# Decoder trunk on one core: where the down product of an expert item stands, how its weight buffers are given back, and in which order items are taken

## The reference, cut to what matters

```python
h = x + hybrid_mixer(rmsnorm(x), ...)            # three head groups and an output product
x = h + hierarchical_moe(rmsnorm(h), ...)
return rmsnorm(x)

# hierarchical_moe, t = 256 tokens of 2048, 4 groups of 8 experts
g_top, g_idx = lax.top_k(softmax(t @ rg_w + rg_b), 1)
e_top, e_idx = lax.top_k(softmax(e_logits), 2)
gate = one_hot(expert_id) * e_w                   # 2 of 32 experts for each token
h = silu(t @ w1[e]) * (t @ w3[e]) * gate[e]       # w1, w3: 2048 x 512
y = sum_e h @ w2[e]                               # w2: 512 x 2048
```

## Time and profile before

| | |
|---|---|
| median of 3 runs | 1461.44 us (1459.39 to 1463.98) |
| the profiled execution | 1461.95 us, its span 1460.2 us |
| mean granted clock of TensorE | 0.915 |
| busy share of the span | PE 82%, DVE 37%, ACT 24%, POOL 16% |
| DMA | 472.17 MB, mean 323 GB/s |

### The profile page before, as it was taken

How to read it: one execution, slowest core, us unless ns; L and a number is a source line. 1 busy time by engine, 2 the same in 40 slices (tenths; PEclk the granted TensorE clock), 3 DMA queues, 4 the chain that set the end, 5 groups by cost and what they waited for, 6 DMA issues and landing times.

```text
span 1460.2 us, 21576 instructions
## 1 busy us (share of the span) xinstructions
PE 1197.6 (82%) x8361; PEld 689.7 (47%) x8361; DVE 533.2 (37%) x1073; ACT 353.1 (24%) x651; POOL 229.7 (16%) x207
## 2 busy tenths in 40 slices
PE   8999999999998666578566667976889788789896
PEld 7874888977774122125112213322243234455563
DVE  6999312344436113114111212313132232344435
ACT  1120477565561101101101010211111111110003
POOL 2002766687860000000000000000000000000000
PEclk9999999999999888869867888999898899999999
DMA  8433444344486999999999999499867779999996
GB/s 210 171 132 139 162 174 172 116 168 139 156 345 268 427 429 429 426 428 427 428 428 426 428 429 426 185 410 428 340 263 329 316 332 422 427 426 430 430 426 286
DMA packets 71566, 472.17 MB, mean 323 GB/s; under 512 B 17329, under 2 KB 17410, under 8 KB 46274
## 3 DMA queue, kind: packets, MB, share of 16 engines
q1 hardware_dynamic: 70834, 469.75, 78.7%
q10 hardware_dynamic: 528, 1.05, 0.2%
q0 software_dynamic: 128, 0.26, 0.1%
HBM read 468.95 MB, written 2.10 MB: 323 GB/s over the span
## 4 chain that ended last, share of the span: by engine, by line
DMA 53%; PE 29%; DVE 2%; ACT 1%; POOL 1%; issue 1%; DVEq 0%; POOLq 0%; ACTq 0%
DMA ring<-in_expert_w_dram 53%; PE ps L1574 11%; PE ps L1916 8%; PE ps L1933 3%; PE ps L1894 2%; PE ps L1925 1%; POOL w_lo L569 1%; PE ps L1841 0%; PE ps L1866 0%; PE ps L1950 0%; DVE reg_x L1502 0%; DVE reg_y L1131 0%; PE ps L1748 0%; PE ps L1696 0%; PE ps L1906 0%
## 5 line engine op out<-in xcount | busy, mean ns | idle before, releaser
L569 POOL TENSOR_TENSOR w_lo<-ring,w_hi 128x512 fp32r<-128x512 f32 x152 | 200.0, 1346 | 72.4 <-ACT w_hi L631 71.2
L1933 PE MATMUL ps<-ring,reg_y 128*32 128x512 f32 x1248 | 174.9, 699 | 38.5 <-POOLq L594 26.7
L1404 DVE TENSOR_TENSOR y_lo_t<-ps,y_hi_t 32x512 fp32r<-32x512 f32 x156 | 107.1, 687 | 205.2 <-ACT y_hi_t L863 201.6
L863 ACT ACTIVATE y_hi_t<-ps 32x512 fp32r<-32x512 f32 x156 | 91.9, 589 | 323.8 <-PE ps L1933 320.9
L1393 DVE TENSOR_SCALAR reg_y<-ps,lamv 128x512 f32<-128x512 f32 x39 | 29.3, 750 | 319.9 <-PE ps L1916 319.9
L1916 PE MATMUL ps<-ring,reg_s 128*32 128x512 f32 x624 | 93.1, 724 | 59.2 <-POOLq L594 59.1
L1916 PE MATMUL ps<-ring,reg_y 128*32 128x512 f32 x624 | 90.2, 696 | 42.5 <-POOLq L594 42.2
L1916 PE MATMUL ps<-reg_e,reg_y 128*32 128x512 f32 x624 | 84.7, 665 | 42.6 <-POOLq L594 42.6
L1916 PE MATMUL ps<-reg_e,reg_s 128*32 128x512 f32 x624 | 86.5, 678 | 38.0 <-POOLq L594 38.0
L631 ACT ACTIVATE w_hi<-ring 128x512 fp32r<-128x512 f32 x152 | 91.6, 630 | 75.8 <-PE ps L1574 66.3
L1933 PEld LDWEIGHTS ps<-ring,reg_y 128*32 128x32 f32 x1248 | 39.3, 120 | 140.0 <-issue 78.1
(11 more groups left out here) (404 smaller groups left out, 1624.0 us busy)
## 6 DMA issues: line engine op xcount, KB each, us to landing
ring<-in_expert_w_dram SPq DMA_DIRECT2D x128, 2048.0 KB, 25.7
reg_e<-in_expert_w_dram SPq DMA_DIRECT2D x64, 2048.0 KB, 25.5
ring<-in_w_in_dram SPq DMA_DIRECT2D x19, 2048.0 KB, 8.1
ring<-in_w_out_dram SPq DMA_DIRECT2D x8, 2048.0 KB, 8.0
reg_x<-in_x_dram SPq DMA_DIRECT2D x4, 1024.0 KB, 8.6
ring<-in_w_in_dram SPq DMA_DIRECT2D x2, 1024.0 KB, 7.4
out_dram<-reg_x SPq DMA_DIRECT2D x3, 512.0 KB, 2.7
reg_e<-in_ssm_w_glu_dram ACTq DMA_DIRECT2D x1, 1024.0 KB, 8.9
```

The costliest lines, as they stand in the source:

```text
L569: G.tensor_tensor(w_lo[:, i % BUFS, :], unit(u % SLOTS_A)[:, c, :], w_hi[:, i % BUFS, :], ALU.subtract).then_inc(row_lo, 1)
L863: A.activation(y_hi_t[SLOT * q:SLOT * q + SLOT, 512 * k:512 * k + 512], psb[3][SLOT * k:SLOT * k + SLOT, :], cp).then_inc(e_yhi, 1)
L1404: V.tensor_tensor(y_lo_t[SLOT * q:SLOT * q + SLOT, w], psb[3][SLOT * k:SLOT * k + SLOT, :], y_hi_t[SLOT * q:SLOT * q + SLOT, w], ALU.subtr ...
L1933: last = M(psb[3][SLOT * i:SLOT * i + SLOT, :], hT[:, 2 * half + f, :], unit2(s)[:, f, 512 * i:512 * i + 512], start=half == 0 and f == 0, ...
```

## The change

There are four edits in the expert stage.

1. `down` of item n-1 no longer follows item n-1's own `turn`. It stands between the two up products of item n: w1 of n, down of n-1, w3 of n, turn of n. It keeps its old place, behind `gather`, at the end of a group and for a single item in the loop. The first item of a group's second block (`pe_item_behind`) has its eight pairs of `combine` behind that `down`, four of them behind `turn`.
2. `slot_free` becomes `w1_free`, `w3_free` and `w2_free`, with two counts for an item each, and `e_in` becomes `w1_in`, `w3_in` and `w2_in`. POOL passes landings on in PE's new order. SP's order of transfers stays.
3. The items that run singly (their number, `n_more` and one, known on the chip) come first, here items 0 to 6; the four fixed groups are items 7 to 38. The first gather and gates are for one item, not eight, and those in the loop too, where before they fetched eight. The last item is now the eighth of a group.
4. POOL clears `y_hi_t` and `y_lo_t` once before the expert stage. DVE's table of item experts (L1345) is put in `y_lo_t`. A small clearing of `selS` moves from the end to before the routing.

```diff
-                    sp.wait_ge(slot_free, n_ * 6 + k + 1)
+                    sp.wait_ge((w1_free, w3_free, w2_free)[k // 2], n_ * 2 + k % 2 + 1)
...
+            g.wait_ge(row_used, ROWS)
+            G.memset(y_hi_t[:, :].bitcast(F), 0.0)
+            G.memset(y_lo_t[:, :].bitcast(F), 0.0).then_inc(y_clear, 1)
...
+            landed(w1_in, 0, 0)
+            landed(w3_in, 2, 0)
             g.wait_ge(rk_ready, 2)
-            with g.Fori(1, ITEMS) as i_:
-                item_landed(g.value_load(ids[0:1, ds(i_, 1)], min_val=0, max_val=NE - 1))
+            more = g.value_load(n_more[0:1, 0:1], min_val=0, max_val=EXTRA - 2)
+            with g.Fori(0, more + 1) as x_:
+                landed(w2_in, 4, expert(x_))
+                e = expert(x_ + 1)
+                landed(w1_in, 0, e)
+                landed(w3_in, 2, e)
+            with g.Fori(0, GROUPS) as it:
+                for q in range(1, QG):
+                    n_ = it * QG + more + (q + 1)
+                    e = expert(n_)
+                    landed(w1_in, 0, e)
+                    landed(w2_in, 4, expert(n_ - 1))
+                    landed(w3_in, 2, e)
...
+            def pe_item_behind(i_, n_, h):
+
+                up(n_, QE * h, 0, (0, 1))
+                down(n_ - 1)
+                up(n_, QE * h, 1, (0,))
+                pe.wait_ge(e_stev, i_)
+                pe.wait_ge(e_ylo, n_ * 4 + 1)
+                combine(i_ - 1, (0, 1))
+                up(n_, QE * h, 1, (1,))
+                combine(i_ - 1, (2, 3))
+                turn(n_)
+                combine(i_ - 1, (4, 5, 6, 7))
                 slots_to_rows(i_, h)
...
+            def pe_group(i0, g_, n0, tail=False):
+                for q in range(QG):
                     n_ = n0 + q
+                    if q == 0:
+                        pe_item(i0, g_, n_)
+                    elif q % QE == 0:
+                        pe_item_behind(i0 + q // QE, n_, q // QE)
+                    else:
+                        up(n_, q, 0, (0, 1))
+                        down(n_ - 1)
+                        up(n_, q, 1, (0, 1))
+                        turn(n_)
+                if not tail:
+                    next_gather(i0 + HG, g_ + 1, QG)
+                    down(n0 + (QG - 1))
...
             pe.wait_ge(id_r, 1)
-            gather(0, QG, BANKS_0, range(0, 10))
+            gather(0, 1, BANKS_0, range(0, 10))
             pe.wait_ge(e_gev, 4)
             up(0, 0, 0, (0,))
...
+            slots_to_rows(0, 0)
+            with pe.If(more > 0):
+                with pe.Fori(0, more) as x_:
+                    next_gather(x_ + 1, x_ + 1, 1)
+                    down(x_)
+                    pe_item(x_ + 1, x_ + 1, x_ + 1)
+            next_gather(more + 1, more + 1, QG)
+            down(more)
+            with pe.Fori(0, GROUPS - 1) as it:
+                pe_group(it * HG + more + 1, it + more + 1, it * QG + more + 1)
+            pe_group(more + ((GROUPS - 1) * HG + 1), more + GROUPS, more + ((GROUPS - 1) * QG + 1), tail=True)
```

More of the change, by code:

```diff
@@ L1437, in v_others @@
[L1437 to L1459, removed]
+            def v_item(i_, n_, q):
+                v_add(i_ - 1, (0, 1, 2, 3))
+                v_up(n_, q)
+                v_add(i_ - 1, (4, 5))
+                v_hidden(n_)
+                v_add(i_ - 1, (6, 7))
+                v_turned(i_)
@@ L1460, in _ @@
+            v_gather(0, 1, BANKS_0, range(0, 5))
             gates()
-            select_weights(0, QG)
-            v_gather(0, QG, BANKS_0, range(5, DC // 2))
+            select_weights(0, 1)
+            v_gather(0, 1, BANKS_0, range(5, DC // 2))
             v_gates(0)
[L1464 to L1477, removed]
+            v_up(0, 0)
+            v_hidden(0)
+            v.wait_ge(y_clear, 1)
@@ new lines, in _ @@
+            item_experts()
+            v_turned(0)
+            more = v.value_load(n_more[0:1, 0:1], min_val=0, max_val=EXTRA - 2)
+            with v.If(more > 0):
+                with v.Fori(0, more) as x_:
+                    next_group(x_ + 1, 1, 1)
+                    v_gather(x_ + 1, 1)
+                    v_gates(x_ + 1)
+                    v_down(x_, 0)
+                    v_item(x_ + 1, x_ + 1, 0)
+            next_group(more + 1, 1, QG)
+            v_gather(more + 1, QG)
+            v_gates(more + 1)
@@ L1479, in v_residual @@
+            v_down(more, 0)
+            with v.Fori(0, GROUPS - 1) as it:
+                v_group(it * HG + more + 1, it + more + 1, it * QG + more + 1)
+            v_group(more + ((GROUPS - 1) * HG + 1), more + GROUPS, more + ((GROUPS - 1) * QG + 1), tail=True)
+            n_last = more + NE
             def v_residual(c):
@@ L1929, in down_half @@
             def down_half(n_, half):
-                s = landed(n_, 4 + half)
+                s = slot_of(4 + half)
+                pe.wait_ge(w2_in, n_ * 2 + half + 1)
                 for f in range(2):
@@ L1982, in next_gather @@
                 pe.wait_ge(e_stev, i_)
-                gather(g_, QG)
-            def next_gates(i_, g_, nq):
+                gather(g_, nq)
                 pe.wait_ge(e_acc, i_ * 8 - 7)
                 gates(g_, nq)
[L1989 to L1992, removed]
+            def pe_group(i0, g_, n0, tail=False):
+                for q in range(QG):
@@ L1993, in pe_items @@
                     n_ = n0 + q
[L1994 to L1998, removed]
-                        next_gates(i_ + 1, g_ + 1, 1 if tail else QG)
-                    down(n_)
-            def pe_group(g_, first=False, tail=False):
-                for h in range(HG):
-                    pe_items(g_ * HG + h, g_, g_ * QG + QE * h, h, first and h == 0, h == HG - 1, tail)
+                    if q == 0:
+                        pe_item(i0, g_, n_)
+                    elif q % QE == 0:
+                        pe_item_behind(i0 + q // QE, n_, q // QE)
+                    else:
+                        up(n_, q, 0, (0, 1))
+                        down(n_ - 1)
+                        up(n_, q, 1, (0, 1))
+                        turn(n_)
```

215 lines of the change are left out of this document (114 added, 101 removed).

## The result

The changed kernel took 1491.28 us (median of 4 runs, 1489.62 to 1493.86) beside 1462.71 us for the kernel before: a ratio of 1.020, 95% interval 1.0175 to 1.0225. The forecast was 1429 us, faster.

A forecast was written before the change was run, and what follows sets the result against it. The expert stage was taken as bound by the DMA stream of weights wherever unbroken. 1461.95 - 40.2 (gaps) + 6.8 (start) + 0.5 (clearing) = 1429.1, so 1429 us was forecast, range 1411 to 1444.

The forecast's parts named there:

- Narrow gathers: Single items' gathers of 32 columns instead of 256: no gain taken, other bound about 6 us less for one gather.
- a period is under 29.4 us: Single items in front: each takes less than an expert's weight stream, which was unbroken with them at the tail.
- The start: Item 0's `down` comes later, so the second expert's w2 lands at 490.3 against 483.5: 6.8 us lost.
- The clearing on POOL: Clearing beside DVE's routing, ahead of the first gather: bounds 0 and 3.8 us, 0.5 us lost taken.
- The gaps: Six breaks in the weight stream behind experts with extra items, 64 us, shrink to 23.8: 40 us saved.
- One that is issued 2.5 us before the last landing L leaves no gap.: A lone weight transfer needs 7.4 us to land; w1 behind items 22, 26 and 30 was thus priced without gap.
- w2 behind items 22 and 30: These items end groups, with the gather before `down`: gap worked out as 1.1 us, 2.0 taken each.
- Behind 18, 24 and 28: Remaining gaps before the next expert's w1 behind these items: 11.8, 6.0 and 2.0 us.
- D: Rival: the shallow queue of half matrices breaks at every expert, 1.5 us x 30 experts, 1474 us; chance 0.05.
- E: Rival: w1 still given back only behind w2's landing, gaps stay, start's loss added: 1469 us; chance 0.03.
- C: Rival: PE bound over items 23 to 30, by late `combine` and half clock after idling: 1439 to 1449 us; chance 0.20.
- B: Rival: narrow gathers fast (-6), clearing free, items 24 and 28 keep half their gaps (-4): 1418 us; chance 0.17.

The follow-up runs named there:

- x1: The changed kernel with all gathers on PE at 256 columns again (`selS` cleared that far): 1446.22 us, 0.9892 of the kernel before.
- x2: The kernel before, with the six gathers of its single items at the end at 32 columns instead of 256: 1500.34 us, ratio 1.0261.
- x3: The changed kernel with 128 columns instead of 32 in the single items' gathers, the first likewise: 1483.40 us, 1.0154 of the kernel before.
- x7: The changed kernel with 192 columns in the single items' gathers: 1449.35 us, 0.9914 of the kernel before.
- x9: x1 with each group item's `down` behind its own `turn` again, as before the change: 1475.40 us, 1.0088 of the kernel before.
- x6: x1 with the first gather alone at 32 columns again: 1456.73 us (10 runs), 0.9954 of the kernel before.

## Why the prediction was wrong, step by step

*The step that failed* is "Narrow gathers", with "I take no gain": it bounded the gain (0 to 6 us) and set no bound on a loss. The pace from the earlier trace rows, 0.12 to 0.13 us a product, is right at the upper level; that the level would hold was assumed. The earlier trace rows show 16 narrow products between wide ones, not 64 in a row behind a wait. Measured, such a gather took 13.3 to 13.8 us, where the prediction's own sign was "still 7.7 us". With it fell "a period is under 29.4 us", taken from a tail with wide gathers: it was 34.9. The narrow gathers cost 45 us (1491.28 to 1446.22): 12.3 at the start, 35.8 with the single items, less 2.8 elsewhere, by the landings. No rival named this. Why the clock stays low during them is not explained here; that the width decides it, x1, x2, x3 and x7 show.

*The start* was sized rightly for the gather that it assumed: in x1 `down` of item 0 begins at 480.0 us, forecast 480.9, and the loss is 7.2, forecast 6.8. The clearing on POOL was not measured alone; this sum leaves it about nothing.

*The gaps* were right in their cause, 27.0 us gained for 40.2. x9 shows that the interleaving gives them. The mis-sized terms:

- "One that is issued 2.5 us before the last landing L leaves no gap." It needs more. w1 behind item 26 was issued at L - 2.3, exactly as worked out:
```profile
1160.92 2.05 SPq L503 DMA_DIRECT2D reg_e<-in_expert_w_dram  x2
```
```profile
reg_e<-in_expert_w_dram SPq DMA_DIRECT2D x1, 2048.0 KB, 9.7
```
 It landed 9.7 us later, at 1170.7, a gap of 2.6. Behind items 22 and 30, with leads of 2.1 and 2.0 us, the gaps are 1.5 and 2.7. Over all sixteen traces, 26 transfers issued 1.75 to 2.75 us ahead landed 4.9 to 7.8 us after the one before (median 5.5), and 143 issued 3.4 to 4.5 ahead had a median of 4.9 and a maximum of 6.4. Three gaps forecast as 0: 6.8 us.
- w2 behind items 22 and 30: 6.5 and 4.2, forecast 2.0 each. Behind 22, 3.03 is the stall and 1.9 the `down` at half clock. Together 6.7 us.
- Behind 18, 24 and 28: 12.9, 6.4 and 3.3 for 11.8, 6.0 and 2.0. Together 2.8 us.

The sum is 16.3. Shorter intervals between the other landings of the stretch give back 3.1, which leaves the 13.2 us missing.

*The rivals.* D, the shallow queue, did not come: transfers land 14.1 us after issue instead of 25.7, and the stretch 8 to 16 takes 236.4 us, before 236.5. E did not: w1 is issued before w2's landing. C's half-clock products come nearest to what happened, but C set them behind idle stretches among items 23 to 30 and at 10 to 20 us. B's fast narrow gathers are the opposite of it.

## What to carry over

Count a product's columns before cutting "useless" ones: where the weight block sets the pace, extra columns were free here (a pair took 0.24 us at 32 columns and at 256), and without them TensorE's clock stayed at its lower level. A cut that gives no gain needs its loss bounded too, by what runs just behind it. When a reordering is bundled with such a cut, time the parts apart: here the interleaving gave 29 us, and the narrow gathers cost 45 and the new order with the counts and the clearing 14.

## What the runs showed of the hardware

- 64 products with 128x128 float32 weight blocks took 7.9 to 9.4 us at 256 columns in x1 (up to 10.7 in other kernels), 9.0 to 10.6 at 192, 12.0 to 13.9 at 128 and 13.3 to 13.8 at 32, all in single items behind a wait. At the upper level a pair takes 0.22 to 0.24 us at either end of these widths, at the lower 0.43.
- Behind an idle of 2.02 us the granted clock was at its lower level for 0 to 6.8 us with 256 columns, 3.4 to 6.8 with 192, 13.7 to 17.1 with 128 and 17.1 to 20.5 with 32, with PE busy from the end of the idle on. A first gather of narrow products without such an idle kept the upper level for 9.4 us once (x6) and fell 1.8 us in once (the changed kernel).
- The level outlasts the narrow products: `down` behind them took 5.5 us instead of 3.5; the clock came back at 600.8, 4.2 us into it.
- A 2048 KB transfer issued about 2 us before the last one in the queue lands left a gap of 0 to 2.9 us (26 cases); issued 3.4 to 4.5 us ahead it left mostly none, at most 1.5 (143 cases).
- PE stood still for 1.6 to 7.6 us near the ends and starts of groups with nothing to wait for. The place moved with the code's, and it stayed with the loop's jump gone; 38 of 47 such stalls hold the start of an instruction packet.
